# Seven block products one pair earlier in two gated layers: form order, sum order and a divided product

## The reference

```python
def swiglu(x, w_in, w_out):
    gate, up = jnp.split(x @ w_in, 2, axis=-1)
    return (jax.nn.silu(gate) * up) @ w_out
...
        h = h + 0.5 * swiglu(rmsnorm(h, ffn1_norm[l]), ffn1_w_in[l], ffn1_w_out[l])
        h = h + hybrid_mixer(...)
        h = h + 0.5 * swiglu(rmsnorm(h, ffn2_norm[l]), ffn2_w_in[l], ffn2_w_out[l])
```

## Time and profile before

| | |
|---|---|
| median of 3 runs | 1612.85 us (1612.77 to 1612.92) |
| profiled execution: its own time | 1612.32 us |
| its span in the trace | 1610.5 us |
| mean granted TensorE clock | 0.999 |
| busy: PE, PEld | 1589.0 us (99%), 1351.1 us (84%) |
| busy: DVE, ACT, POOL | 966.2 us (60%), 761.2 us (47%), 886.7 us (55%) |

### The profile page before, as it was taken

How to read it: one execution, slowest core, us unless ns; L and a number is a source line. 1 busy time by engine, 2 the same in 40 slices (tenths; PEclk the granted TensorE clock), 3 DMA queues, 4 the chain that set the end, 5 groups by cost and what they waited for, 6 DMA issues and landing times.

```text
span 1610.5 us, 23966 instructions
## 1 busy us (share of the span) xinstructions
PE 1589.0 (99%) x9196; PEld 1351.1 (84%) x9196; DVE 966.2 (60%) x1592; ACT 761.2 (47%) x1391; POOL 886.7 (55%) x641
## 2 busy tenths in 40 slices
PE   9999999999999999999999999999999999999997
PEld 8787878888888888889998887877767889999886
DVE  7176756884444225878884434576783587886224
ACT  6366655543344324545554323577573445555222
POOL 7424354575445553558889553654114548889650
PEclk9999999999999999999999999999999999999999
DMA  5411103322323222323333222322012323233221
GB/s 209 151 53 53 40 14 105 117 93 93 104 92 104 93 95 76 105 93 105 105 106 105 93 95 74 120 93 80 27 28 92 99 98 105 96 103 106 96 100 53
DMA packets 49682, 147.56 MB, mean 92 GB/s; under 512 B 5152, under 2 KB 13728, under 8 KB 49568
## 3 DMA queue, kind: packets, MB, share of 16 engines
q1 hardware_dynamic: 48232, 143.39, 26.8%
q10 hardware_dynamic: 1336, 2.63, 0.5%
HBM read 142.84 MB, written 3.41 MB: 91 GB/s over the span
## 4 chain that ended last, share of the span: by engine, by line
PE 81%; DVE 2%; POOL 1%; ACT 1%; issue 1%; DMA 1%; SPq 0%; DVEq 0%; ACTq 0%
PE PS L621 14%; PE PS L623 14%; PE PS L622 14%; PE PS L2154 7%; PE PS L2155 6%; PE PS L2156 6%; PE PS L1413 4%; PE PS L582 4%; PE PS L1424 3%; PE PS L590 2%; PE PS L1074 2%; PE PS L1096 2%; PE PS L1121 1%; POOL w_lo L683 1%; DMA stage<-in_weights 1%
## 5 line engine op out<-in xcount | busy, mean ns | idle before, releaser
L683 POOL TENSOR_TENSOR w_lo<-stage,w_hi 128x512 fp32r<-128x512 f32 x402 | 567.3, 1438 | 598.6 <-ACT w_hi L657 597.7
L657 ACT ACTIVATE w_hi<-stage 128x1024 fp32r<-128x1024 f32 x262 | 270.5, 1054 | 303.3 <-DMA stage<-in_weights 289.4
L621 PE MATMUL PS<-H_hi,w_hi 128*128 128x512 f32 x512 | 199.4, 389 | 0.4 <-DVE rcol L1622 0.4
L622 PE MATMUL PS<-H_lo,w_hi 128*128 128x512 f32 x512 | 199.3, 389 | 0.0
L623 PE MATMUL PS<-H_hi,w_lo 128*128 128x512 f32 x512 | 199.2, 389 | 0.0
L621 PE MATMUL PS<-A_hi,w_hi 128*128 128x512 f32 x496 | 193.2, 389 | 0.6 <-DVE A_lo L829 0.6
L623 PE MATMUL PS<-A_hi,w_lo 128*128 128x512 f32 x496 | 193.0, 389 | 0.0
L622 PE MATMUL PS<-A_lo,w_hi 128*128 128x512 f32 x496 | 193.0, 389 | 0.0
L2128 POOL TENSOR_TENSOR S_lo<-S_f,S_hi 128x512 fp32r<-128x512 f32 x90 | 126.5, 1421 | 66.5 <-DVE S_f L1988 37.7
L2128 POOL TENSOR_TENSOR w_lo<-stage,w_hi 128x512 fp32r<-128x512 f32 x90 | 141.8, 1603 | 0.0
L2154 PE MATMUL PS<-F,w_hi 128*128 128x256 f32 x480 | 137.5, 287 | 1.7 <-ACT conv L2047 1.1
(11 more groups left out here) (295 smaller groups left out, 3583.2 us busy)
## 6 DMA issues: line engine op xcount, KB each, us to landing
stage<-in_weights SPq DMA_DIRECT2D x254, 512.0 KB, 3.4
stage<-in_weights SPq DMA_DIRECT2D x32, 128.0 KB, 2.8
out_t<-Y SPq DMA_DIRECT2D x8, 256.0 KB, 2.0
X<-in_x_t SPq DMA_DIRECT2D x3, 512.0 KB, 8.4
bias_line<-bias_line ACTq DMA_DIRECT2D x1, 1270.0 KB
strip<-bias_line ACTq DMA_DIRECT2D x1, 1024.0 KB, 5.0
stage<-in_weights SPq DMA_DIRECT2D x2, 256.0 KB, 4.1
V<-QF SPq DMA_DIRECT2D x4, 128.0 KB, 2.7
```

The source lines that it names most:

```text
L621: pe.matmul(out, a, h_hi, start=first, stop=False, skip_group_check=skip)
L622: pe.matmul(out, a, h_lo, start=False, stop=False, skip_group_check=skip)
L657: act.activation(w_hi[:, slot, :], stage[:, slot, :], ACT.Copy).then_inc(hi_done, 1)
L683: lo = pool.tensor_tensor(w_lo[:, slot, cols], stage[:, slot, cols], w_hi[:, slot, cols].bitcast(F32), ALU.subtract)
```

## The change

`PLAIN` goes from 7 to 6: pair 6 becomes a fast pair in both layers. The seven forms are put in the order in which PE comes to them, and PE waits for each form by itself (`form_ready`) where it waited for all seven at once. ACT waits for as many of the blocks and form sums as each form needs (`FORMED`). On DVE, the lo parts of B11, T1, T2 stand where the first three stood; then, behind the evacuation of pair 4, stand `A11_lo` and all four sums of pair 6, and behind them the lo parts of B21 and T3; T4 stands behind the evacuation of pair 5, and B22 in `dve_fast` behind `A11_lo` of pair 7. In the last pair (21) the 12 matmuls of p2 stand in two parts of 6, ahead of p7 and behind it.

```diff
-PLAIN = 7
+PLAIN = 6
...
                 elif inst and n == 4:
-                    dve_forms_lo(dve, inst, range(3, 7))
-                elif inst and n == 5:
                     dve_corner_lo(dve, inst, u_up, PLAIN)
                     for k in range(4):
                         dve_sum(dve, inst, u_up, PLAIN, k)
+                    dve_forms_lo(dve, inst, range(3, 5))
+                elif inst and n == 5:
+                    dve_forms_lo(dve, inst, range(5, 6))
...
-        FORMS = [(F1, B11_HI, B11_LO), (F1, B21_HI, B21_LO), (F1, B22_HI, B22_LO), (F2, T1_HI, T1_LO),
-                 (F2, T2_HI, T2_LO), (F2, T3_HI, T3_LO), (F1, T4_HI, T4_LO)]
+        FORMS = [(F1, B11_HI, B11_LO), (F2, T1_HI, T1_LO), (F2, T2_HI, T2_LO), (F1, B21_HI, B21_LO),
+                 (F2, T3_HI, T3_LO), (F1, T4_HI, T4_LO), (F1, B22_HI, B22_LO)]
+        FORMED = [8, 9, 11, 8, 10, 12, 8]
...
-                fast.formed.wait(act, inst, 8 if k < 3 else 12)
+                fast.formed.wait(act, inst, FORMED[k])
...
                 if more:
                     dve_corner_lo(dve, inst, u_up, n + 1)
+                    if n == PLAIN:
+                        dve_forms_lo(dve, inst, range(6, 7))
                     dve_sum(dve, inst, u_up, n + 1, 0)
...
-            fast.form_lo.wait(pe, inst, 7)
+            def form_ready(n, form):
+
+                if n == PLAIN:
+                    fast.form_lo.wait(pe, inst, form + 1)
+
+            form_ready(PLAIN, 0)
             p1(PLAIN)
...
-                product_of(corner("a", n), *unit_half(ug, 1), 1, True).then_inc(unit_done, 1)
+                form_ready(n, 3)
+                last = n + 1 == FC
+                p2 = product_of(corner("a", n), *unit_half(ug, 1), 3, True, range(2 if last else 4))
+                if not last:
+                    p2.then_inc(unit_done, 1)
                 fast.sum_lo.wait(pe, inst, q + 3)
                 fast.snapped.wait(pe, inst, q + 2)
-                product_of(corner("b", n), *sum_parts(n, 2), 5, False).then_inc(fast.spent.sem, 1)
+                form_ready(n, 4)
+                product_of(corner("b", n), *sum_parts(n, 2), 4, False).then_inc(fast.spent.sem, 1)
+                if last:
+                    product_of(corner("a", n), *unit_half(ug, 1), 3, False, range(2, 4)).then_inc(unit_done, 1)
                 if n + 1 < FC:
                     p1(n + 1)
```

More of the change, by code:

```diff
@@ L1932, in dve_form_sums @@
         def dve_form_sums(dve, inst):
-            b11, b21, b22, t1, t2, t3, t4 = [form_f(k) for k in range(7)]
+            b11, t1, t2, b21, t3, t4, b22 = [form_f(k) for k in range(7)]
             b12 = F1_f[:, B12_F, :, :]
@@ L2147, in pe_fast, with product_of @@
         def pe_fast(pe, inst, u_up):
-            def product_of(bank, hi, lo, form, first):
+            def product_of(bank, hi, lo, form, first, ks=range(4)):
                 where, h, l = FORMS[form]
-                for k in range(4):
+                for k in ks:
                     cols = bass.ts(k, P)
@@ L2187, in pe_fast @@
                 bank_free("c", n, 4)
-                product_of(corner("c", n), *sum_parts(n, 0), 3, True).then_inc(fast.spent.sem, 1)
+                form_ready(n, 1)
+                product_of(corner("c", n), *sum_parts(n, 0), 1, True).then_inc(fast.spent.sem, 1)
                 fast.sum_lo.wait(pe, inst, q + 2)
                 fast.snapped.wait(pe, inst, q + 1)
-                product_of(corner("b", n), *sum_parts(n, 1), 4, False).then_inc(fast.spent.sem, 1)
+                form_ready(n, 2)
+                product_of(corner("b", n), *sum_parts(n, 1), 2, False).then_inc(fast.spent.sem, 1)
                 pe.wait_ge(lo_done, ug + 1)
                 bank_free("a", n, 1)
-                product_of(corner("a", n), *unit_half(ug, 1), 1, True).then_inc(unit_done, 1)
+                form_ready(n, 3)
[3 more added lines that the diff above has]
+                    p2.then_inc(unit_done, 1)
                 fast.sum_lo.wait(pe, inst, q + 3)
                 fast.snapped.wait(pe, inst, q + 2)
-                product_of(corner("b", n), *sum_parts(n, 2), 5, False).then_inc(fast.spent.sem, 1)
+                form_ready(n, 4)
+                product_of(corner("b", n), *sum_parts(n, 2), 4, False).then_inc(fast.spent.sem, 1)
+                if last:
+                    product_of(corner("a", n), *unit_half(ug, 1), 3, False, range(2, 4)).then_inc(unit_done, 1)
                 if n + 1 < FC:
@@ L2201, in pe_fast @@
                 fast.snapped.wait(pe, inst, q + 3)
-                product_of(corner("b", n), *unit_half(uv, 1), 6, False).then_inc(fast.spent.sem, 1)
+                form_ready(n, 5)
+                product_of(corner("b", n), *unit_half(uv, 1), 5, False).then_inc(fast.spent.sem, 1)
                 fast.block.wait(pe, inst, 4 * (n - PLAIN) + 2)
-                product_of(corner("c", n), *unit_half(uv, 0), 2, False).then_inc(unit_done, 1)
+                form_ready(n, 6)
+                product_of(corner("c", n), *unit_half(uv, 0), 6, False).then_inc(unit_done, 1)
         @block.sync
```

## The result

The changed kernel takes 1617.58 us (median of 7 runs, 1617.28 to 1618.39) against 1612.83 us of the kernel before (7 runs, 1612.56 to 1613.44) on the same chip: 1.003 times the time, with a 95% interval of 1.002 to 1.0041. It is slower, by 4.75 us. The forecast was 1616.5 us in a range of 1612.2 to 1618.2, with the main case, a stall ahead of p4 of pair 6 in both layers.

A forecast was written before the change was run, and what follows sets the result against it. PE, busy 99% of the span, bounds the kernel, following a POOL, DVE and ACT round of 10.33 us. A +2.85 and B +1.05 give +3.9, taken as +3.7 on 1612.3: 1616.0, plus 0.5 for the median, 1616.5 us; range 1612.2 to 1618.2.

The forecast's parts named there:

- (b): One gap ahead of p4 of pair 6, 2.9 to 4 us in A, 1 to 2.5 in B, released by ACT's L2049.
- (d): Sign in the profile: no gap of 0.72 us in the last pair.
- (e): Sign in the profile: DVE's L1944 at 1.2 us, not 2.3.
- (a): Last plain matmul starts near 700.9 in A's own clock; matmuls of a fast pair keep 0.12 us.
- (1): Pair 6 fast in place of plain, each layer: 10.88 - 10.06, -0.82 us.
- (2): p2 in two parts in the last pair, filling the 0.72 us gap: -0.68 us a layer.
- (3): p4's gaps of 0.27 us in pairs 7 to 9 and 0.17 more in pair 10: +0.95 us a layer.
- (4): Fast part starting one pair earlier, stall ahead of p4 of pair 6: 3.4 us in A, 1.6 in B.
- (c): Sign in the profile: p4 to p4 10.33 us from pair 6 on.
- rival with all turns lost: "The turns come out worse": all five lost in both layers, or PE also waits in pair 7; 1619 us, chance 0.08.
- the new order fits: Round starts in time, sum 1 of pair 7 before 708.5, no p4 stall: 1612.3 to 1609.9, chance 0.16.
- only layer A stalls: In B DVE waits for PE at pair 5, so the start may come in time: 1615.4, chance 0.14.

The follow-up runs named there:

- Experiment 3: Changed kernel with POOL's three `w_lo` of pair 6 replaced by memsets to zero, which read nothing from SBUF: 1611.57 us, ratio 0.999.
- experiment 6: Changed kernel with "keep u3" ahead of the hi part of sum 1 in ACT's list: 1616.13 us, ratio 1.0019.
- experiment 1: Kernel before, `PLAIN` still 7, with only p2 of the last pair in two parts of 6 matmuls: 1611.72 us, ratio 0.9992.
- experiment 2: Changed kernel with p2 of the last pair whole again: 1618.61 us, ratio 1.0035.
- experiment 9: Changed kernel, PE making p1 of pair 7 twice in layer A, 12 matmuls more: 1616.99 us, ratio 1.0026.
- experiment 5: Changed kernel, PE making p1 of pair 7 three times in layer A, 24 matmuls more: 1617.94 us, ratio 1.0032.
- experiment 4: Kernel before with only `PLAIN = 6`, old order of forms, PE waiting for all seven: 1627.9 us, ratio 1.0091.
- experiment 8: Kernel of experiment 1 with POOL's lo parts of the sums in the order 0, 2, 1: 1607.01 us, ratio 0.9963.
- experiment 7: Changed kernel with POOL's lo parts of the sums in the order 0, 2, 1: 1611.43 us, ratio 0.999.
- experiment 10: Kernel of experiment 7 with p1 of pair 7 made twice in layer A: 1610.47 us, ratio 0.9985.

## Why the prediction was right, and where it was off

**What was right.** The mechanism, its place and nearly all of its size. With 0.80 us taken off for the profile's offset, layer A's walk has sum 3 end at 698.75 (forecast 698.7), sum 1 of pair 7 at 711.9 (712.0), p4 start at 712.94 (713.2); with 4.26 us taken off, layer B's has 1309.0 (1309.0), 1322.4 (1322.4) and 1323.4 (1323.6). The stalls are 3.19 and 1.47 us against 3.4 and 1.6. Four turns were lost in A and three in B, as said. Checks (b), (d) and (e) hold, but for the releaser in (b): the profile names none ("issue"), and only the starts show ACT's L2049 0.5 us ahead. Of (a) the first half holds (the last plain matmul at 701.69 - 0.80 = 700.89); the second half, 0.12 us for all matmuls, fails in pair 6 of layer A. Layer B came out at +0.98 against +1.05. Experiment 3 takes the turns away and the stall goes with them; experiment 6 shows that the lateness is the round's.

**Steps, by term.** (1) the pair of -0.82 us was not measured by itself; it is in the sums of both layers, which close with it. (2) The divided product: -0.68 forecast; 0.67 and 0.63 us by the layers' lengths in experiment 1, 0.72 and 0.64 in experiment 2. (3) +0.95 (3 x 0.27 + 0.17 is 0.98) held in layer B, and in A only once the clock was kept: experiment 9 has +2.78 us in A (from 701.65 to 869.90 us is 168.25, less 165.47), against my +2.85. (4) right within 0.2 us. With (2) at -0.65 the layers close: B is -0.82 - 0.65 + 0.98 + 1.47 = +0.98; A, with no gaps up to pair 10, is -0.82 - 0.65 + 3.19 + 1.56 = +3.28, measured +3.29.

**What was missing.** The clock. My sum priced an idle PE by its idle time alone, "at a clock of 0.999 all along", and looked no further. Behind 3.19 us of idle time some 17 matmuls ran at the lower level, which cost 1.56 us. The net is smaller, +0.5 to 0.6 us, since in that time POOL, DVE and ACT went on and won the slack that I had said they never win back: check (c) fails in A, where p4 to p4 is 11.64 us, then 10.08 to 10.12, and 10.32 from pair 10 on. Rounds shorter than 10.33 us behind the gap were one of the signs of a wrong prediction that I had named, and layer A shows it. The sentence "a delay of this round at its start is never made good" needs the addition: unless PE is held up by something else meanwhile. Experiments 5 and 9 bear that out, where the clock was kept and the rounds are 10.3 us from pair 6 on. So layer A is +3.29 in place of +2.85, and that it is no farther off is in part luck: of two terms that I did not have, +1.56 for the clock and -0.98 for the slack, the second takes back most of the first.

**Misread and misadded.** That "all seven form parts" show the turns lost is not so: the first three were held, at 2.27 us each, and the other four took 1.15 us each with POOL idle. And the rival with all turns lost, 3.3 us on the main case of 1616.5, is 1619.8 us and not 1619. Neither touches the sum.

**The account.** Forecast for the profiled execution +3.7; measured +5.26, of it 0.44 from layer A's clock, -0.07 from B, 0.2 that I had taken off the sum, 0.17 between the layers, and 0.8 of start offset. Median against median it is 4.75 us; the time, 1617.58 us, is 1.1 us above the forecast. Of the rivals, "the new order fits" and "only layer A stalls" are out by the rows. "The turns come out worse" is out too: four and three turns were lost, and the extra came from the clock.

**What stays open.** Whether the longer wait ahead of layer B in experiment 5 belongs to that program or to that execution: the profiled execution is 0.7 us above the median and has a lower mean clock than the median one, which speaks for the execution, but there is one trace of it only. What keeps experiment 5's other executions from gaining what layer A gained is open with it. And at what idle time the clock falls: the low stretch came behind 3.19, 3.21, 2.85, 2.24 and 1.93 us, and not behind 2.86 (experiment 4, layer B), 2.12, 1.94, 1.74 and 1.47. In experiment 4 one execution has both, 2.85 us with a fall and 2.86 us without, so the length of the gap alone doesn't decide.

## What to carry to other kernels

Before starting a cheaper stage earlier, walk the engine that prepares it (here DVE) instruction by instruction from the last fixed event to the first product that needs its result, and add a turn for each of its two-input SBUF instructions that meets a POOL instruction reading SBUF; that walk gave both stalls within 0.2 us. Price a stall of PE of about 2 us or more with the slow matmuls that may follow (1.56 us here), and not only with its length, and ask how much of that the other engines win back. And look at what the steady round is made of before moving its start: one exchange in POOL's order was worth 4.7 us with the old start, where the earlier start cost as much. The fastest kernel of all (experiment 8, 1607.01 us) has the old start.

## What the runs showed of the hardware that was not expected

A single core's PE, at the upper clock for the whole kernel otherwise, fell to the lower one for about 3.4 us behind one idle time of 3.2 us (0.213 us in place of 0.120 for 256 columns). The fall came 0.1 us after PE had taken up work again in the changed kernel, and 0.8 to 1.1 us after it in experiments 2, 4 and 5. 24 useless matmuls in that idle time kept it up. So did 12, which left 1.74 us of it. It stayed up behind 2.12 us in experiment 6, and fell behind 2.24 us in experiment 7, where another gap of 0.85 us lay 8 us ahead. In experiment 4 it fell behind 2.85 us in layer A and not behind 2.86 us in layer B. Added work on the bounding engine made a layer shorter: layer A by 0.51 us in experiment 9 and by 1.26 us in experiment 10, in the profiles (by 0.6 and 0.96 us in the medians, the first with overlapping intervals).
